# Values of an attention stage: from moving operand to stationary operand in two column halves of TensorE

## The chip, the cores and the metric

The kernel runs on one core of one Trainium2 chip. The metric is the time of one execution on the device, in microseconds (us). The kernel before takes 1840.47 us (median of 3 runs, 1840.46 to 1841.13).

## The reference, cut to what matters

One decoder block over 1024 tokens of width 1024, all in float32. Two token mixers run in parallel and are merged by gates; a feed-forward part follows.

```python
q_a, ..., q_b, k_b, v_b, iq, ik, iw, g_merge = split(rmsnorm(h) @ w_in)
# NSA: 8 heads in 2 groups of 4 that share keys and values
o_cmp = softmax(q @ kc) @ vc              # 63 compressed keys
o_slc = softmax(q @ k_selected) @ v_sel   # 8 blocks of 64 keys, chosen per query
o_win = softmax(q @ k_win) @ v_win        # the last 512 keys
y_a = g0 * o_cmp + g1 * o_slc + g2 * o_win
# DSA: 8 heads, one key and one value, 256 keys chosen per query
y_b = softmax(q_b @ k_chosen) @ v_chosen
merged = sigmoid(gA) * (y_a @ w_nsa) + sigmoid(gB) * (y_b @ w_dsa)
h = h + merged @ w_out
h = h + (silu(hn @ w_gate) * (hn @ w_up)) @ w_down
out = rmsnorm(h)
```

Selected keys are computed as dense attention with a bias of -1e30 on keys that aren't chosen.

## The kernel before, in words

The program is written by hand for each engine: every engine has its own list of instructions, and counting semaphores join them. Five stages follow one another: the input projection with the choice of DSA keys (until some 496 us), the attention (496 to 954 us), the merge, the output projection, and the feed-forward part. Only the attention and the first steps of the merge are touched.

The attention walks over 192 units. A unit is one branch (dsa, win or slc), one tile of 128 queries `i` (0 to 7), and one of 8 heads. It has n key blocks of 128 keys: n = i + 1, at most 5 for win. Summed over all units that is 816 key blocks. The loop `for u in range(STEPS6)` is written out on every engine in the same order, and each part of a unit happens a fixed number of steps later:

- step u: TensorE computes the scores of unit u into one half of `psA` (lines 1401 and 1402: the keys come as a high and a low part, each one pass). VectorE scales them, adds the bias and takes the maximum (line 1949, tile `s`).
- `E_LAG` = 1 step later: ScalarE takes the exponential and its sum (line 1188, tile `p`).
- `T_LAG` = 2: TensorE turns the n blocks of probabilities (line 1342, a transpose: the data is the stationary operand and `ident` moves) into one of two banks of `psT`, up to 4 blocks a bank. ScalarE or VectorE copies a bank to `pT` (line 602). `group` makes TensorE wait until the bank used two groups ago has been copied.
- `V_LAG` = 3: TensorE multiplies by the values (line 1517). Stationary is a block of `pT`, 128 keys by 128 queries, and the 64 columns of values move. Each such product in float32 is two instructions in the trace, each with its own weight load. All 8 heads of a query tile lie side by side in one bank of `psT`, queries on the partitions.
- `F_LAG` = 4: after the last head VectorE divides by the sums (line 1977), and GpSimd adds the branches (line 987). `Y_LAG` = 7: the sum is turned (line 1342, from `ya`) and split into a high part `yTh` by ScalarE (line 1178) and a low part `yTl` by VectorE (line 2008).

Interleaved with the units stand the compression of keys (line 1526, 64 products of 128 by 128), the scores and the output of the compressed branch for each tile (lines 1549, 1550 and 1562), and the ranking of blocks on VectorE and GpSimd. The merge has 16 steps (`m_step`), each 24 instructions with 512 moving columns; the first stands in the loop's tail, the others behind it. Step m serves output columns m // 2 and token half m % 2.

Of the kernel before, what the change touches and what calls it, by code (L numbers as in the profile page):

```python
# [28 lines left out]
F32 = mybir.dt.float32  # L29
# [7 lines left out]
P = 128  # L37
HD = 64
# [10 lines left out]
def hybrid_block(nc, A, out, scratch):  # L49
# [62 lines left out]
    v_win = sb(mix, "v_win", [P, NT, KV * HD])  # L112
    nsa_gate = sb(mix, "nsa_gate", [P, NT, 3 * H])
# [55 lines left out]
    yTh, yTl = {}, {}  # L169
    for set_ in ("nsa", "dsa"):  # L170
        yTh[set_] = sb(att, f"yTh_{set_}", [P, KT // 2, S], F32R)
        yTl[set_] = sb(att, f"yTl_{set_}", [P, KT // 2, S], F32R)
    with ExitStack() as s:
        w1c = [sb(s, f"cmp_w1_{n}", [P, JP, HH * P]) for n in "kv"]
    kT = {a: sb(att, f"kT_{a}", [P, KV, 2, S], F32R) for a in ("slc", "win")}
    work = ExitStack()
    s_sb = [sb(work, f"s{n}", [P, S]) for n in range(2)]
# [3 lines left out]
    PR = 3  # L181
    p_sb = [sb(work, f"p{n}", [P, S]) for n in range(PR)]
    pT = [sb(work, f"pT{n}", [P, NT, P]) for n in range(2)]
    ya = [sb(work, f"ya{n}", [P, H * HD]) for n in range(2)]
    yt = sb(work, "ytmp", [P, H * HD])
    c_s = sb(work, "c_s", [P, H, 64])
    c_p = sb(work, "c_p", [P, H, 64])
    c_pT = sb(work, "c_pT", [P, 4, P])
# [4 lines left out]
    cmp_a = sb(work, "cmp_above", [P, KV, NSLC, NSLC])  # L193
    cmp_b = sb(work, "cmp_equal", [P, KV, NSLC, NSLC])
# [6 lines left out]
    psum_r = sb(work, "psum_r", [P, 3, NT, H])  # L201
    work.close()
# [130 lines left out]

    Z_STEPS, G_STEPS = 8 * len(ORDER), 4 * KT
    free1 = [8 * (n // 4) + 7 if n < NCH else Z_STEPS + 2 * (n - NCH) + 1 for n in range(len(items1))]
    M_STEPS, O_STEPS, F_STEPS = 2 * KT, 2 * NT, FT
    free2 = [2 * j + 1 for j in range(KT)] + [M_STEPS + 8 * (n // 4) + 7 for n in range(8)]
# [73 lines left out]
    W2_AT = [ND + 64, ND + 72]  # L411
# [11 lines left out]
    E_LAG, T_LAG, V_LAG, F_LAG, Y_LAG = 1, 2, 3, 4, 7  # L423
    STEPS6 = len(units) + Y_LAG + 2

# [17 lines left out]


    groups6, opened = [], []
    for u in range(STEPS6):
        a, i, h = at(u - T_LAG)
        if a:
            groups6 += [("p", u - T_LAG, g) for g in range(len(seg(keys_of(a, i)[1])))]
        a, i, h = at(u - V_LAG)  # L450
        if a and h == 0:
            opened.append((a, i))
# [4 lines left out]
        for key, stage in (("cs", 0), ("cp", C_TURN), ("co", C_OUT)):  # L457
            if cmp_tile(u, stage) is not None:
                groups6.append((key, cmp_tile(u, stage), 0))
        if y_of(u):  # L460
            groups6.append(("y", *y_of(u)))
# [3 lines left out]
    def by_act(key):  # L465
        return key[0] in ("ch", "cp") or (key[0] == "p" and key[2] == 0)
# [3 lines left out]
    o_took = nth(opened)  # L470
    ysteps = nth([k for k in groups6 if k[0] == "y"])
    groups_y = list(ysteps)

# [25 lines left out]
    pv_ps, o_out, y_done, yh_done = sem("pv_ps"), sem("o_out"), sem("y_added"), sem("yh")  # L499
# [38 lines left out]
    w2.gone = [(m_ps, 2 * j + 2) for j in range(KT)]  # L538
# [38 lines left out]
    N_CONST1 = 9  # L577
    N_CONST6 = N_CONST1 + 2 + 11

    def windows(eng, n, done):  # L580

        for g in range(KV):
            src = kcvcT[HD * g:HD * (g + 1), n, :].rearrange("p (c s) -> p s c", s=CSTR)
            for u in range(2):
                for j in range(2):
                    last = eng.tensor_tensor(
                        xc[n][HD * u:HD * (u + 1), 8 * j:8 * j + 8, g, 0:NW], src[:, u::2, j:j + NW],
                        posc[n][HD * g:HD * (g + 1), CSTR * j + u:CSTR * (j + 1):2].unsqueeze(2).to_broadcast([HD, 8, NW]),
                        ALU.add)
                    last.then_inc(done, 1)  # L590

    def evac_p(eng, copy, v, act_side):

        a, i, h = at(v)
        for g, (c0, c1) in enumerate(seg(keys_of(a, i)[1])):
            key = ("p", v, g)
            if by_act(key) != act_side:
                continue
            eng.wait_ge(t_ps, g6[key] + 1)
            if v >= 2:  # L600
                eng.wait_ge(pv_ps, v - 1)
# [9 lines left out]
    def _(sp):  # L611
# [106 lines left out]
        for n in range(2 * RAW, RAW + RING):  # L718
            w2.load(sp, n)
# [1614 lines left out]
```

## Time and profile before

| | |
|---|---|
| median of 3 runs | 1840.47 us |
| the profiled execution | 1840.48 us |
| its span, first to last instruction | 1838.8 us |
| TensorE busy (matmuls) | 1707.3 us, 93% |
| VectorE, ScalarE, GpSimd busy | 66%, 38%, 31% |
| granted TensorE clock, mean | 0.97 |

A row of the profile names line, engine, operation, written tile <- read tiles, and shape. PE is TensorE's matmul side and PEld its weight loads, DVE is VectorE, ACT is ScalarE, POOL is GpSimd, SP is SyncE, which issues the DMAs. The ends of matmuls are modelled, and their intervals overlap, so what a matmul costs is read from the distance between starts. PEclk is the granted clock as a share of 2.4 GHz: 0.5 is 1.2 GHz.

### The profile page before, as it was taken

To read this page: it belongs to the slowest core of one execution; us is meant where nothing else is said; L and a number is where in the kernel's file an instruction comes from. 1 tells how busy PE (TensorE), PEld (TensorE's weight loads), DVE (VectorE), ACT (ScalarE), POOL (GpSimd) and SP (SyncE) were. 2 spreads that over 40 slices of the span, in tenths; PEclk is the share of its full clock that TensorE was granted. 3 is DMA by queue.
4 is the path that set the end of the run, shared out by engine and by line. 5 is a ranking of instruction groups with operands and counts; after the bars stand their busy time and mean duration, and the time that the engine had idled before them with its cause. 6 is when DMAs were issued, how large, how long until landed. Compare 5 with 4: busy or idle time off the path is not lost.

```text
span 1838.8 us, 25573 instructions
## 1 busy us (share of the span) xinstructions
PE 1707.3 (93%) x9248; PEld 1467.2 (80%) x9248; DVE 1208.7 (66%) x2181; ACT 701.4 (38%) x1398; POOL 567.1 (31%) x396
## 2 busy tenths in 40 slices
PE   6789989999999999999999999899999999889994
PEld 5667778888898989889988877688888888668883
DVE  6689778999243545566646516667676676458976
ACT  5543433311274457655532114422322222234443
POOL 3303232322040012322212121544454445245451
PEclk9899989999999989999999999999999999989997
DMA  5103232532242001001015523122333222853432
GB/s 178 46 12 105 71 102 73 174 92 91 50 136 115 13 24 47 12 13 35 1 44 163 169 90 120 50 94 87 123 117 104 86 87 75 297 200 98 156 102 92
DMA packets 152590, 172.21 MB, mean 94 GB/s; under 512 B 18961, under 2 KB 102929, under 8 KB 152209
## 3 DMA queue, kind: packets, MB, share of 16 engines
q1 hardware_dynamic: 152464, 170.57, 28.9%
q8 instruction: 75, 1.23, 0.3%
q14 instruction: 51, 0.41, 0.1%
HBM read 121.00 MB, written 49.55 MB: 93 GB/s over the span
## 4 chain that ended last, share of the span: by engine, by line
PE 78%; DVE 10%; ACT 3%; DMA 3%; issue 3%; POOL 1%; SPq 1%; DVEq 0%; ACTq 0%; POOLq 0%
PE psA L1335 13%; PE psA L1336 13%; PE psA L1337 13%; PE psT L1517 9%; PE psT L1342 7%; PE psT L1336 5%; PE psT L1337 5%; PE psT L1335 5%; PE psA L1402 3%; PE psA L1401 3%; DMA act_raw<-scratch_act 1%; DVE rotated L1776 1%; DVE equal L1836 1%; POOL w_lo L377 1%; DVE above L1836 1%
## 5 line engine op out<-in xcount | busy, mean ns | idle before, releaser
L377 POOL TENSOR_TENSOR w_lo<-w_raw,w_hi 128x1024 fp32r<-128x1024 f32 (+2 forms) x52 | 119.9, 2314 | 243.3 <-ACT w_hi L372 243.3
L1188 ACT ACTIVATE p<-s,nmax 128x640 f32<-128x640 f32 (+7 forms) x192 | 143.9, 750 | 121.4 <-DVE nmax L1949 120.8
L995 POOL TENSOR_TENSOR w_lo<-w_sum,w_hi 128x1024 fp32r<-128x1024 f32 x44 | 115.5, 2626 | 129.4 <-ACT w_hi L1243 129.4
L1342 PE MATMUL psT<-ident,p 128*128 128x128 f32 x816 | 131.2, 282 | 19.2 <-DVE yTl_dsa L2008 4.7
L1018 POOL TENSOR_TENSOR w_lo<-act_raw,w_hi 128x512 fp32r<-128x512 f32 x77 | 104.9, 1366 | 137.8 <-ACT w_hi L1272 137.8
L2161 DVE TENSOR_TENSOR w_lo<-wd,w_hi 128x512 fp32r<-128x512 f32 x77 | 96.5, 1257 | 66.9 <-ACT w_hi L1279 66.6
L1335 PE MATMUL psA<-w_hi,xTh 128*128 128x512 f32 (+2 forms) x320 | 124.5, 389 | 13.6 <-POOL w_lo L377 9.5
L1336 PE MATMUL psA<-w_lo,xTh 128*128 128x512 f32 (+2 forms) x320 | 120.4, 376 | 0.0
L1337 PE MATMUL psA<-w_hi,xTl 128*128 128x512 f32 (+2 forms) x320 | 120.1, 375 | 0.0
L1342 PEld LDWEIGHTS psT<-ident,p 128*128 128x128 f32 x816 | 98.8, 154 | 26.4 <-ACT p L1188 7.0
L372 ACT CAST w_hi<-w_raw 128x1024 fp32r<-128x1024 f32 (+2 forms) x52 | 52.3, 1014 | 151.0 <-PE psA L1337 108.9
L1272 ACT CAST w_hi<-act_raw 128x512 fp32r<-128x512 f32 x77 | 47.8, 621 | 151.7 <-PE psA L1337 57.2
L602 ACT COPY pT<-psT 128x512 f32<-128x512 f32 (+3 forms) x192 | 93.8, 489 | 20.7 <-PE psT L1342 20.6
L1335 PE MATMUL psA<-xTh,w_hi 128*128 128x512 f32 x256 | 100.0, 391 | 0.0
L1337 PE MATMUL psA<-xTh,w_lo 128*128 128x512 f32 x256 | 99.6, 389 | 0.0
L1336 PE MATMUL psA<-xTl,w_hi 128*128 128x512 f32 x256 | 99.6, 389 | 0.0
L602 DVE COPY pT<-psT 128x128 f32<-128x128 f32 (+3 forms) x96 | 40.8, 425 | 82.9 <-PE psT L1342 82.5
L1836 DVE TENSOR_SCALAR_CACHE_REDUCE equal<-score,bit_try 128x512 f32<-128x512 f32 (+2 forms) x93 | 93.8, 1009 | 0.0
L1243 ACT CAST w_hi<-w_sum 128x1024 fp32r<-128x1024 f32 x44 | 46.2, 1053 | 118.1 <-DVE w_sum L2103 58.1
L894 POOL TENSOR_TENSOR roped<-z,cosT 128x512 f32<-128x512 f32 (+3 forms) x48 | 40.3, 846 | 163.4 <-ACT z L1063 96.8
L2117 DVE TENSOR_TENSOR act<-gate,act 128x512 f32<-128x512 f32 x33 | 67.0, 2029 | 35.1 <-ACT gate L1283 35.1
L1335 PE MATMUL psA<-w_hi 128*128 128x512 f32 x176 | 71.5, 406 | 17.3 <-DVE w_lo L2161 11.5
(351 smaller groups left out, 4949.1 us busy)
## 6 DMA issues: line engine op xcount, KB each, us to landing
act_raw<-scratch_act SPq DMA_DIRECT2D x77, 256.0 KB, 2.6
w_raw<-in_w_in_dram SPq DMA_DIRECT2D x28, 512.0 KB, 3.8
scratch_act<-act SPq DMA_DIRECT2D x33, 256.0 KB, 2.1
scratch_act<-act_sum SPq DMA_DIRECT2D x33, 256.0 KB, 2.1
scratch_gates<-gate_out SPq DMA_DIRECT2D x32, 256.0 KB, 3.1
gates<-scratch_gates SPq DMA_DIRECT2D x32, 256.0 KB, 4.1
wd<-in_w_down_dram SPq DMA_DIRECT2D x4, 1536.0 KB, 7.7
a<-in_w_gate_dram SPq DMA_DIRECT2D x22, 256.0 KB, 3.2
```

The lines of the kernel that those rows point to most:

```text
L377: nc.gpsimd.tensor_tensor(self.lo[n % RING][:, 0:u], self.raw[n % RAW][:, 0:u], self.hi[n % RING][:, 0:u].bitcast(F32), ALU.subtract).then ...
L602: copy(pT[v % 2][:, c0 // P:c1 // P, :].rearrange("p k t -> p (k t)"), psT[:, g6[key] % 2, 0:c1 - c0])\
L995: nc.gpsimd.tensor_tensor(lo2[n % RING][:], block_of(n)[:], hi2[n % RING][:].bitcast(F32), ALU.subtract)\
L1018: nc.gpsimd.tensor_tensor(lo2[slot][:, 0:512], act_raw[n % 6][:], hi2[slot][:, 0:512].bitcast(F32), ALU.subtract)\
L1188: a_.activation(p_sb[v % PR][:, 0:n], s_sb[v % 2][:, 0:n], ACT.Exp, scale=-1.0, bias=nmax[:, BR[a], i, h:h + 1], accum_out=psum_p[:, BR[a] ...
L1335: pe.matmul(ps, ah, bh, start=first, stop=False)
L1336: pe.matmul(ps, ah, bl, start=False, stop=False)
L1337: mm = pe.matmul(ps, al, bh, start=False, stop=last)
L1342: mm = pe.transpose(bank[:, P * n:P * (n + 1)], src, ident[:])
L1517: mm = pe.matmul(bank[:, HD * h:HD * (h + 1)], pT[v % 2][:, k, :], val, start=(k == 0), stop=(k == n - 1))
L1836: done.append(signal(v_.tensor_scalar((tk_gt, tk_eq)[n % 2][:, 0:P * (i + 1)], score_of(i), threshold(n), None, ALU.is_ge, ALU.add, accum_ ...
L2161: v_.tensor_tensor(lo2[slot][:, 512:1024], wd_of(D_FROM[q])[:, k, :], hi2[slot][:, 512:1024].bitcast(F32), ALU.subtract).then_inc(dl_done, 1)
```

## The change

The order of operands in the product with the values is exchanged. The 64 columns of values are stationary, and fill one half of TensorE's columns. The turned probabilities of two neighbouring heads, 2 x 128 queries, move as 256 columns. Even key blocks use columns 0 to 63 and write partitions 0 to 63, odd ones use columns 64 to 127 and write partitions 64 to 127. The outcome is the sum over even and over odd blocks, with the head's dimension on the partitions. So it has to be turned back: ScalarE copies the bank of 4 heads to `acc`, TensorE turns 4 blocks, VectorE scales both halves into `ytmp`, and GpSimd adds the halves.

```diff
-    E_LAG, T_LAG, V_LAG, F_LAG, Y_LAG = 1, 2, 3, 4, 7
+    E_LAG, T_LAG, V_LAG = 1, 3, 1
+    O_LAG, F_LAG, Y_LAG = T_LAG + 1 + V_LAG + 1, T_LAG + 1 + V_LAG + 2, 8
+    M_AT = [len(units) + T_LAG, len(units) + O_LAG, len(units) + Y_LAG + 1]
...
+    for u in range(1, len(units), 2):
+        a, i, h = units[u]
+        n = keys_of(a, i)[1]
+        mine = [(u, k, min(2, n - k)) for k in range(0, n, 2)]
+        first = (len(mine) + 1) // 2
+        for m, job in enumerate(mine):
+            jobs_at[u + T_LAG + (m >= first)].append(len(jobs))
+            jobs.append(job)
...
         for u in range(STEPS6):
+            for j in jobs_at[u]:
+                (a, i, h), k, nk, w = of_job(j)
+                uq = jobs[j][0]
+                pe.wait_ge(p_done, uq + 1)
+                turn4(group(("p", j, 0)), [s_sb[v % SR][:, P * c:P * (c + 1)] for c in range(k, k + nk) for v in (uq - 1, uq)])\
+                    .then_inc(t_ps, 1)
...
-            v = u - V_LAG
-            a, i, h = at(v)
-            if a:
+            for j in jobs_at[u - V_LAG]:
+                (a, i, h), k, nk, w = of_job(j)
...
-                for k in range(n):
...
-                    mm = pe.matmul(bank[:, HD * h:HD * (h + 1)], pT[v % 2][:, k, :], val, start=(k == 0), stop=(k == n - 1))
-                mm.then_inc(pv_ps, 1)
+                for c in range(k, k + nk):
...
+                    rows, cols = slice(HD * (c % 2), HD * (c % 2 + 1)), slice(2 * P * (c - k), 2 * P * (c - k + 1))
+                    mm = pe.matmul(bank[rows], val, pT[j % PT][:, cols], start=(c < 2), stop=(c >= n - 2))
+                if n == 1:
+                    mm = pe.matmul(bank[HD:P], zero[:], pT[j % PT][:, 0:2 * P], start=True, stop=True)
+                mm.then_inc(pj_done, 1)
...
+            if group_of(u, O_LAG):
+                o = o6[group_of(u, O_LAG)]
+                pe.wait_ge(acc_out, o + 1)
+                turn4(group(("o", *opened[o])), [acc[o % 2][:, P * k:P * (k + 1)] for k in range(G)]).then_inc(t_ps, 1)
+            if u == M_AT[1]:
+                m_step(1)
...
-            v_.tensor_tensor(heads(target[:], H), ps, r, ALU.mult).then_inc(o_out, 1)
+            v_.tensor_tensor(yt[o % 2][:].rearrange("p h r d -> p h (r d)"),
+                             psT[:, g6[key] % 2, :].rearrange("p (h c) -> p h c", h=G), r, ALU.mult).then_inc(t_dve, 1)
```

A job is the turning and copying of up to two key blocks of two heads, at most 512 columns; ScalarE copies the even jobs and VectorE the odd ones. A pair's jobs are shared out over two steps. What else changes: the exponential writes over `s`, now 6 buffers; `pT` has 8. For the second half of the tokens ScalarE copies the turned sum raw to `y_raw`, and splits it at the end into `yTh` and `yTl` in 4 pieces for each mixer. The merge begins with three steps of the first token half (`MSEQ`). SyncE no longer waits for the last product before it loads the merge's gates, but only for the last output of the compressed branch and the last ranking. GpSimd builds the compression's inputs in four pieces inside the loop.

In TensorE's list, two steps of slc units in query tile 7 (n = 8) read as follows before. `p` are probabilities, `ident` the unit matrix, `kT_slc` keys, `pT` turned probabilities.

```order
L1342 MATMUL psT<-ident,p2 128x128 x8
L1401 MATMUL psA<-kT_slc,q1 128x512
L1402 MATMUL psA<-kT_slc,q1 128x512
L1401 MATMUL psA<-kT_slc,q1 128x512
L1402 MATMUL psA<-kT_slc,q1 128x512
L1517 MATMUL psT<-v_slc,pT0 128x64 x8
L1342 MATMUL psT<-ident,p0 128x128 x8
```

At the same place in the changed kernel the end of a step and the start of the next read as follows; `s` holds the probabilities.

```order
L1474 MATMUL psA<-kT_slc,q1 128x512
L1589 MATMUL psT<-pT0,v_slc 64x256 x2
L1589 MATMUL psT<-pT1,v_slc 64x256 x2
L1414 MATMUL psT<-ident,acc1 128x128 x4
L1414 MATMUL psT<-ident,s0 128x128
L1414 MATMUL psT<-ident,s1 128x128
L1414 MATMUL psT<-ident,s0 128x128
L1414 MATMUL psT<-ident,s1 128x128
```

Where a step had 8 products with 64 moving columns, it has 4 with 256 (two jobs of two key blocks, for two heads); behind every second pair stand 4 further transposes, of `acc`, and then the next step's begin.

The loop's tail in TensorE's list before, behind the last scores (`w2_hi0` is the first merge weight):

```order
L1342 MATMUL psT<-ident,p1 128x128 x8
L1517 MATMUL psT<-v_slc,pT1 128x64 x8
L1342 MATMUL psT<-ident,p2 128x128 x8
L1517 MATMUL psT<-v_slc,pT0 128x64 x8
L1517 MATMUL psT<-v_slc,pT1 128x64 x8
L1335 MATMUL psA<-yTh_nsa,w2_hi0 128x512
```

And in the changed kernel, from the end of the first merge step to the start of the second:

```order
L1409 MATMUL psA<-yTh0_dsa,w2_lo0 128x512
L1589 MATMUL psT<-pT4,v_slc 64x256 x2
L1589 MATMUL psT<-pT5,v_slc 64x256 x2
L1589 MATMUL psT<-pT6,v_slc 64x256 x2
L1589 MATMUL psT<-pT7,v_slc 64x256 x2
L1414 MATMUL psT<-ident,acc1 128x128 x4
L1407 MATMUL psA<-yTh0_nsa,w2_hi1 128x512
```

The first merge step moved ahead of the last values, and the second ahead of the last sum `ya`, whose four transposes stand between the second and the third.

## Rows read from the trace of the kernel before

**Rows 1.** The page: busy time, slices, and the chain by line.

```profile
PE 1707.3 (93%) x9248; PEld 1467.2 (80%) x9248; DVE 1208.7 (66%) x2181; ACT 701.4 (38%) x1398; POOL 567.1 (31%) x396
...
PE psA L1335 13%; PE psA L1336 13%; PE psA L1337 13%; PE psT L1517 9%; PE psT L1342 7%; PE psT L1336 5%; PE psT L1337 5%; PE psT L1335 5%; PE psA L1402 3%; PE psA L1401 3%; DMA act_raw<-scratch_act 1%; DVE rotated L1776 1%; DVE equal L1836 1%; POOL w_lo L377 1%; DVE above L1836 1%
```

**Rows 2.** Engines' busy time in stretches of the attention; PEclk follows the engines.

```profile
496.00:540.00 44.00, 41.22 (x311) 39.42 (x312) 20.79 (x76) 34.65 (x103) 23.59 (x29) 0.92 0.60 157
540.00:658.00 118.00, 111.59 (x907) 106.05 (x907) 56.55 (x118) 56.21 (x109) 2.09 (x2) 1.00 0.14 55
658.00:700.00 42.00, 39.63 (x295) 38.76 (x294) 21.69 (x88) 26.45 (x99) 7.96 (x7) 0.84 0.06 17
700.00:948.00 248.00, 239.53 (x1937) 228.53 (x1935) 145.84 (x360) 143.86 (x308) 52.05 (x76) 0.99 0.06 20
```

**Rows 3.** TensorE in time, units of n = 8: start, length, line, shape, count.

```profile
936.13 0.40 PE L1402 MATMUL psA<-kT_slc,q 128*128 128x512 f32 x1
936.36 1.90 PE L1517 MATMUL psT<-v_slc,pT 128*128 128x64 f32 x16
938.09 1.05 PE L1342 MATMUL psT<-ident,p 128*128 128x128 f32 x8
938.90 0.47 PE L1401 MATMUL psA<-kT_slc,q 128*128 128x512 f32 x1
939.21 0.39 PE L1402 MATMUL psA<-kT_slc,q 128*128 128x512 f32 x1
939.43 0.39 PE L1401 MATMUL psA<-kT_slc,q 128*128 128x512 f32 x1
939.67 0.40 PE L1402 MATMUL psA<-kT_slc,q 128*128 128x512 f32 x1
939.90 1.90 PE L1517 MATMUL psT<-v_slc,pT 128*128 128x64 f32 x16
941.63 1.05 PE L1342 MATMUL psT<-ident,p 128*128 128x128 f32 x8
942.52 1.90 PE L1517 MATMUL psT<-v_slc,pT 128*128 128x64 f32 x16
```

**Rows 4.** Groups of the attention by shape: busy us, mean ns, then idle before.

```profile
L1342 PE MATMUL psT<-ident,p 128*128 128x128 f32 x816 | 131.2, 282 | 19.2 <-DVE yTl_dsa L2008 4.7 <-DVE yTl_nsa L2008 4.7 <-DVE ya L1984 3.1
L1517 PE MATMUL psT<-v_slc,pT 128*128 128x64 f32 x576 | 74.1, 275 | 0.0
L1517 PE MATMUL psT<-v_b,pT 128*128 128x64 f32 x576 | 73.3, 273 | 0.0
L1517 PE MATMUL psT<-v_win,pT 128*128 128x64 f32 x480 | 63.6, 275 | 0.0
L602 DVE COPY pT<-psT 128x512 f32<-128x512 f32 x16 | 11.1, 692 | 18.3 <-PE psT L1342 18.3
L602 ACT COPY pT<-psT 128x512 f32<-128x512 f32 x120 | 68.2, 568 | 12.9 <-PE psT L1342 12.9
L1977 DVE TENSOR_TENSOR ytmp<-psT,psum_r 128x512 f32<-128x512 f32 x16 | 11.0, 686 | 2.6 <-PE psT L1517 2.6
```

**Rows 5.** The chain of waits, 544 to 563 us: a long piece of 128 instructions.

```profile
547.42 14.36 PE psT L1526 x128
```

**Rows 6.** TensorE in time: products with 64 moving columns in one pass.

```profile
625.12 0.28 PE L1550 MATMUL psT<-k_cmp,q 128*128 128x64 f32 x1
625.23 0.28 PE L1549 MATMUL psT<-k_cmp,q 128*128 128x64 f32 x1
```

**Rows 7.** All engines in time, the loop's tail: TensorE's wait behind the first merge step.

```profile
954.22 0.60 PE L1342 MATMUL psT<-ident,ya 128*128 128x128 f32 x4
954.85 0.58 ACT L1178 CAST yTh_nsa<-psT 128x512 fp32r<-128x512 f32 x1 [9.37 <-PE psT L1342]
955.47 0.69 DVE L2008 TENSOR_TENSOR yTl_nsa<-psT,yTh_nsa 128x512 fp32r<-128x512 f32 x1 [5.87 <-ACT yTh_nsa L1178]
956.22 0.50 PE L1335 MATMUL psA<-yTh_nsa,w_hi 128*128 128x512 f32 x1 [1.40 <-DVE yTl_nsa L2008]
```

More of the change, by code:

```diff
@@ L332, in hybrid_block @@
     tg = {k: n for n, k in enumerate(tgroups)}
+    MSEQ = [(j, 0) for j in range(3)] + [(j, 1) for j in range(3)]
+    MSEQ += [(j, half) for j in range(3, KT) for half in range(2)]
+    m_last = [MSEQ.index((j, 1)) for j in range(KT)]
     Z_STEPS, G_STEPS = 8 * len(ORDER), 4 * KT
@@ L442, in y_of, with group_of @@
         return (a, i) if a in ("slc", "dsa") and h == H - 1 else None
+    def group_of(u, lag):
+        a, i, h = at(u - lag)
+        return (a, i, h // G) if a and h % G == G - 1 else None
+    jobs, jobs_at = [], {u: [] for u in range(-1, STEPS6)}
+    last_job, pair_jobs = {}, {}
+    for u in range(1, len(units), 2):
[6 more added lines that the diff above has]
+            jobs.append(job)
+        last_job[a, i, h // G] = pair_jobs[u - 1] = pair_jobs[u] = len(jobs) - 1
     groups6, opened = [], []
     for u in range(STEPS6):
-        a, i, h = at(u - T_LAG)
-        if a:
[L449 to L452, printed above, removed]
+        groups6 += [("p", j, 0) for j in jobs_at[u]]
         if u == CH_AT:
@@ L537, in hybrid_block @@
             w1.gone.append((g_ps, 2 * (n - NCH) + 2))
-    w2.gone = [(m_ps, 2 * j + 2) for j in range(KT)]
+    w2.gone = [(m_ps, m + 1) for m in m_last]
     frees = 0
@@ L575, in heads, with windows, of_job @@
         return ap.rearrange("p (h d) -> p h d", h=n)
-    N_CONST1 = 9
+    N_CONST1 = 10
     N_CONST6 = N_CONST1 + 2 + 11
-    def windows(eng, n, done):
+    def windows(eng, n, u, done):
         for g in range(KV):
             src = kcvcT[HD * g:HD * (g + 1), n, :].rearrange("p (c s) -> p s c", s=CSTR)
[L584 to L592, printed above, removed]
-        a, i, h = at(v)
[L595 to L601, printed above, removed]
-            copy(pT[v % 2][:, c0 // P:c1 // P, :].rearrange("p k t -> p (k t)"), psT[:, g6[key] % 2, 0:c1 - c0])\
-                .then_inc(t_act if act_side else t_dve, 1)
+            for j in range(2):
+                eng.tensor_tensor(
+                    xc[n][HD * u:HD * (u + 1), 8 * j:8 * j + 8, g, 0:NW], src[:, u::2, j:j + NW],
+                    posc[n][HD * g:HD * (g + 1), CSTR * j + u:CSTR * (j + 1):2].unsqueeze(2).to_broadcast([HD, 8, NW]),
+                    ALU.add).then_inc(done, 1)
+    def of_job(j):
+        u, k, nk = jobs[j]
+        return units[u], k, nk, nk * 2 * P
     def roped(q, col, w):
@@ L963, in _ @@
         for u in range(STEPS6):
+            if u in X_AT:
+                n, r = X_AT.index(u) // 2, X_AT.index(u) % 2
+                if any(group_of(v, F_LAG) for v in range(u)):
+                    pool.wait_ge(y_done, sum(1 for v in range(u) if group_of(v, F_LAG)))
+                windows(nc.gpsimd, n, r, (cx_k, cx_v)[n])
+                pool.wait_ge((cx_k, cx_v)[n], 4 * (r + 1))
+            if u == MASKS_AT:
+                block_masks()
             i = cmp_tile(u, C_MAX)
@@ L1152, in _, with chunks_hi @@
             a_.activation(gst[g % 2][:], psA[:, g % 4, :], ACT.Sigmoid).then_inc(g_out, 1)
+        def chunks_hi(set_):
+            act.wait_ge(pj_done, len(jobs))
+            act.wait_ge(t_act, act_took["y", "dsa" if set_ == "dsa" else "slc", NT - 1])
+            for k in range(KT // 2):
+                a_.copy(yTh[set_, 1][:, k, :], y_raw[set_][:, k, :]).then_inc(yc_hi, 1)
         for u in range(STEPS6):
```

313 lines of the change are left out of this document (182 added, 131 removed).

## The prediction

> **What bounds the kernel now.** I read the page's busy times and chain first. TensorE is busy for 93% of the span, and the products with the values alone make 9% of the chain, the transposes 7% [rows 1]. Then the stretches: from 496 to 948 us TensorE's busy time is 432 of 452 us, while VectorE has 245, ScalarE 261 and GpSimd 86 [rows 2]. A busy PE includes some waiting, so I took the steps apart. In units of n = 8 one step, from value products to value products, takes 939.90 - 936.36 = 3.54 us: 1.73 for 16 value instructions (108 ns each), 0.81 for 8 transposes, 1.00 for four score products [rows 3]. Nothing stands between them. So TensorE's own work sets the pace there, and what the change does to its list decides. In that step ScalarE has one copy of 0.57 us of `pT`, VectorE one of 0.69 [rows 4], beside one exponential and one bias pass; both are covered.
>
> **Value products that go.** 576 + 576 + 480 = 1632 instructions [rows 4] by 108 ns (16 in 938.09 - 936.36) [rows 3]: -176.3 us. What do they wait for? One-pass products with the same 64 moving columns start every 110 ns [rows 6], so that distance is not the moving columns: it is the load of 128 stationary columns. The change halves the stationary side, which makes loads cheap, and lengthens the moving side to 256.
>
> **Value products that come.** 408 products and 12 with `zero` are 840 instructions, if each is two as before. Price of one with 256 columns: full float32 with 128 columns takes 14.36 / 128 = 112 ns [rows 5], and there weight load and moving side can't be told apart. The upper bound is proportional to the columns, 224 ns, which also stands next to the one-pass product of 512 columns, 939.67 to 939.90, 0.23 us [rows 3]. The lower bound is that 112 ns were all weight load, and 256 columns cost no more than that. I take 224, since two streams of 256 are one of 512. (The Trainium skill, FP8 and Floating Point Precision, section TensorE Precision Notes, has four passes for true FP32. With two instructions that is two passes in each, 512 columns, and the sum would be as with 224.)
>
> **How far the halves overlap.** If a product in one half runs beside one in the other, with starts in the list's order, a product waits only for the one before it in its own half. In a job of two blocks the list reads even, even, odd, odd (two instructions each): three time slots in place of four; two jobs in a step take five in place of eight. Counted through all 232 jobs in 168 steps that is 588 slots in place of 840. 588 x 0.224 = +131.7 us. No row shows two column halves at once, so both ends stay: 588, and 840, which is +188.2.
>
> **Sums turned back.** 48 groups of 4 transposes = 192, by 111 ns (8 in 942.52 - 941.63) [rows 3]: +21.3 us. The copies to `acc` (48 on ScalarE at some 0.57 us, a copy of this shape [rows 4]) and 48 scalings in place of 24 on VectorE at 0.69 [rows 4] lie beside TensorE, but the transposes' bank must be free. Where a step behind such a group has two jobs (n of 5 and more: 12 query tiles, 2 groups each, 24 times), the second job waits until VectorE has scaled: 0.69 us and some 0.1 of signals, of which the first job's transposes cover 0.44. 24 x 0.36 = +8.6 us. If VectorE is held up elsewhere it is double that; none if TensorE has slack there.
>
> **Changing the array's shape.** The value products now use half the columns, everything around them all. 168 steps have such products, so 336 changes of shape. The trace has none: all rows read 128*128. Below is nothing. Above: TensorE runs empty each time. A value instruction's row lasts 275 ns, of which the next hides all but 108, so emptying costs at most 167 ns [rows 3, 4]. The nearest rows are the change from transposes to plain products: 938.90 to 939.21, 0.31 us, where the next of the same kind needs 0.22 to 0.24; back from plain products to transposes the distance stays at the usual 108 ns [rows 3]. One direction costs about 0.07, the other nothing. I take that here: 168 x 0.07 = +11.8 us (0 to +56).
>
> **Waits that go.** TensorE waited 4.7 + 4.7 us for `yTl` [rows 4], about 0.8 a time; for the second token half only ScalarE's copy remains before the bank is free: -4.7. In the tail it stood 1.40 us for the last `yTl` [rows 7], and the start of the next merge step was stretched; three steps of the first half, 5.5 us each, now cover the last transposes, splits and the gates' loads: -2. The clock stood at 0.92 and 0.84 of full in 496 to 540 and 658 to 700 us [rows 2], so 16% of 44 us and 32% of 42 us at half of full speed, 20 us in all, of which 10 are lost. These are units of n = 1, where every engine waits for another. More steps of slack (`T_LAG` 3, six `s`) fill some of it, fewer value products empty it again: -4, anything from -10 to +8. Together about -11.
>
> **Taken as free.** ScalarE has at n = 8 for a pair two exponentials, two copies and half an `acc`, VectorE two bias passes, two copies and half a scaling; by the rows above both come to some 4.3 us of a pair's 6 us. GpSimd has 3 small additions for each of 32 groups and one for 16, in steps where it is idle. The raw copies and later splits of the second half move 16 VectorE and ScalarE operations to the tail, beside 11 us of merge steps. GpSimd's window pieces end before step 36 needs them. SyncE issues the gates' loads earlier, when the DMA queues are nearly empty (0.06 [rows 2]).
>
> **Sum.** -176.3 + 131.7 + 21.3 + 8.6 + 11.8 - 11 = -13.9 us. The profiled execution took 1840.48 us, the same as the median of the runs, so the sum gives 1826.6, and I say 1827. Its own range, with the switch from 0 to 0.07 in both directions and the clock's term at either end, is 1805 to 1845.
>
> **Rivals.**
> - *Every change of shape empties TensorE.* The place is each border between scores, value products and transposes, 336 in all, at 167 ns [rows 3, 4]: +56 in place of +11.8, so 1871, slower. It decides from about 0.08 us a change, where the sum crosses zero. For it speaks that weights of the one shape can hardly be loaded among products of the other. Against it, that a change of kind is free one way and cheap the other [rows 3]. (The Trainium skill, TensorEngine Tiling, section Tiling Modes, says that changing the tiling mode drains TensorE, and changing the tile does not. By that rule this rival is the forecast; no row of the trace can show it.) Chance 24%.
> - *The halves don't overlap*, because the products queue or because float32 doesn't allow it: 840 slots, +56.4, so 1883. The values then cost more than before, 188 against 176. (The Trainium skill, TensorE: Matmul & The Clock Gate, Part 3, measured three column tiles at 2.38 times one; it tells nothing of float32.) Chance 8%.
> - *256 columns cost what a load costs*, 112 ns: 588 x 0.112 = 65.9, so 65.8 less than taken, 1761. For it speaks only that rows 5 don't exclude it. Chance 10%.
> - *TensorE gets its time and loses it again to the two banks.* Every job, sum and `ya` goes through two banks of `psT`, and half of the jobs now depend on VectorE, which also has the ranking. At 0.08 us for each of 168 steps that is +13.4, so 1840, no change. For it speaks that VectorE already makes TensorE wait for `ya` and `yTl` [rows 4]; against it that a copy takes 0.57 to 0.69 us of a step of some 3. Chance 14%.
>
> **Numbers.** The forecast has 44%. A measurement of this kernel can't tell less than 0.2%, 3.7 us, from no change. Faster by more: 40 of the forecast's 44, all 10 of the cheap columns, 4 of the two banks, 54%. Within: 2 of the forecast, 2 of the emptying, 6 of the banks, 10%. Slower: 2, 22, 8 and 4, 36%. The range of eight in ten leaves out the cheap columns below and the case without overlap above, and runs from 1785 to 1876.
>
> **What would show it.** In the changed profile: value instructions of 256 columns whose starts in pairs (even beside odd) lie 0 to 10 ns apart, and some 224 ns in one half; five slots, 1.1 us, in a step of n = 8, which then takes 2.9 to 3.1 us against 3.54. From a score product to the first value product, and from the last one to the first transpose, no more than 0.07 us above the usual distance; 0.17 or more at each would show the first rival. Starts 224 ns apart throughout: no overlap. Behind `acc`'s transposes a wait for VectorE's scaling of about 0.4 us at n of 5 and more. Attention's end, 954 us now, at 941; the merge and all behind it shifted as a whole. What would make it wrong: a price of the shape's change above 0.08 us, or stretches at half clock that grow past 20 us because the units of n = 1 and 2 give TensorE less to do.

## The result, and the profile after

| kernel | median us | runs | ratio to before, 95% interval |
|---|---|---|---|
| before | 1840.8 | 1840.46 to 1845.89 (4) | 1 |
| changed | 1860.2 | 1859.06 to 1862.78 (4) | 1.0101 [1.0088, 1.0114] |

The change makes the kernel slower by 1.0%, some 19 us. I had forecast 1827, a gain of 14. The page of the changed kernel, first its busy times, then the chain by line:

```profile
PE 1707.2 (92%) x8648; PEld 1356.7 (73%) x8648; DVE 1257.4 (68%) x2225; ACT 700.5 (38%) x1378; POOL 604.8 (32%) x461
...
PE psA L1407 13%; PE psA L1408 13%; PE psA L1409 13%; PE psT L1414 8%; PE psT L1589 6%; PE psT L1408 5%; PE psT L1407 5%; PE psT L1409 5%; PE psA L1474 3%; PE psA L1473 3%; DMA act_raw<-scratch_act 1%; DVE rotated L1855 1%; DVE equal L1915 1%; POOL w_lo L390 1%; DVE above L1915 1%
```

The products with the values (L1589) fell from 9% of the chain to 6%, and the transposes (L1414) rose from 7% to 8% [rows 1]. VectorE has 49 us more, GpSimd 38. The same stretches as in [rows 2], with busy time and count of PE, PEld, DVE, ACT and POOL, and behind them the granted clock:

```profile
496.00:540.00 44.00, 39.96 (x234) 25.56 (x233) 24.00 (x83) 28.19 (x81) 25.12 (x24) 0.92 0.56 145
540.00:658.00 118.00, 111.25 (x780) 81.58 (x779) 64.00 (x127) 61.34 (x121) 10.94 (x22) 1.00 0.16 59
658.00:700.00 42.00, 34.59 (x258) 24.82 (x257) 22.75 (x85) 23.39 (x76) 11.48 (x15) 1.00 0.04 14
700.00:948.00 248.00, 227.76 (x1486) 157.42 (x1484) 166.59 (x372) 137.15 (x303) 74.10 (x115) 0.99 0.08 24
```

TensorE was busy for 432 us of these 452 before and is for 414 now. It waits. What for, in all of 490 to 1062 us (total, times, longest; an idle time of 150 ns or less isn't listed):

```profile
PE psT L1414 <- DVE ya L2058: 10.2, 8, 2.7
PE psT L1414 <- DVE ytmp L2050: 10.0, 20, 0.6
PE psA L1407 <- DVE merged L2085: 5.8, 2, 4.3
PE psT L1589 <- DVE pT L2120: 4.6, 9, 0.6
PE psT L1414 <- ACT acc L1237: 3.9, 8, 0.9
```

Before, the largest entries were 4.7 twice, for `yTl`, and 3.1 for `ya` [rows 4]. All of TensorE's listed waits from the first score product to the first output projection add up to 44.9 us, before to 21.8; those of the transposes alone to 31.9, before to 19.0. One step of n = 8, TensorE in time (the last two rows belong to the next one):

```profile
946.48 0.63 PE L1414 MATMUL psT<-ident,s 128*128 128x128 f32 x4 [0.50 <-DVE ytmp L2050]
...
947.64 0.40 PE L1474 MATMUL psA<-kT_slc,q 128*128 128x512 f32 x1
947.97 1.08 PE L1589 MATMUL psT<-pT,v_slc 128*64 128x256 f32 x8
948.99 1.09 PE L1414 MATMUL psT<-ident,s 128*128 128x128 f32 x8
949.84 0.48 PE L1473 MATMUL psA<-kT_slc,q 128*128 128x512 f32 x1
```

From values to values (947.97 to 950.94, where the next ones start) it takes 2.97 us, 3.54 before [rows 3]: the gain is there where n is large. Within the eight value instructions the records start at 943.879 and 943.885, 944.146 and 944.152, 944.362 and 944.368, 944.578 and 944.584 (the step before this one), and the next transpose at 944.894. So two halves run side by side, 6 to 7 ns apart. A pair follows a pair after 216 ns, the first after 267. The way in and the way out of the halves are longer than usual: score to value 327 ns where it was 232, value to transpose 310 where two pairs lie 216 apart. And the transpose behind that one is late as well: it starts at 945.060, 166 ns on, where transposes usually follow each other after 109. Leaving out waits and half clock, this second distance is 165 ns behind 145 of 146 stretches in the halves; before, it was that long behind 10 of 149.

I took the distance from each TensorE instruction to the next one, between the first score product and the first output projection, and added it up by the kind of the earlier one (sums over the trace's records, us; the differences are of unrounded sums):

| kind | before | changed | difference |
|---|---|---|---|
| value products | 186.6 | 132.8 | -53.8 |
| scores (way into the halves) | 120.9 | 141.1 | +20.2 |
| transposes | 108.8 | 150.8 | +41.9 |
| merge steps | 88.7 | 96.7 | +8.1 |
| rest | 37.8 | 39.8 | +1.9 |
| all | 542.9 | 561.1 | +18.3 |

A wait stands in this table under the kind ahead of it. The first stage, whose code is the same, took 2.6 us more in this profiled run, what lies behind the output projection's start 1.4.

The merge, too, lost its cover. TensorE in time, the fifth merge step's first product:

```profile
992.02 0.77 PE L1407 MATMUL psA<-yTh_nsa,w_hi 128*128 128x512 f32 x1 [4.30 <-DVE merged L2085]
```

VectorE there: the last four subtractions, and the first operation of the third merge result:

```profile
976.33 2.50 DVE L2065 TENSOR_TENSOR yTl_nsa<-y_raw_nsa,yTh_nsa 128x512 fp32r<-128x512 f32 x4 [3.02 <-ACT yTh_nsa L1204]
...
989.86 0.69 DVE L2080 TENSOR_TENSOR ma<-psA,gates 128x512 f32<-128x512 f32 x1 [7.44 <-DMA gates<-scratch_gates]
```

SyncE's issues:

```profile
981.30 0.37 SPq L378 DMA_DIRECT2D w_raw<-in_w_branch_nsa_dram  x1
...
982.81 1.93 SPq L739 DMA_DIRECT2D gates<-scratch_gates  x4
```

VectorE makes the second merge result only behind the eight subtractions, the gates of the third step are asked for at 982.8 behind a weight load, and the 4.30 us of waiting end in a stretch at half clock (989.8 to 996.6, 1.2 GHz in place of 2.4). Merge steps 2 to 4 take 25.0 us; before, three took 16.5, and the only wait above 0.3 us was the 1.40 [rows 7].

### The profile page after: what moved, and what is told of

Its sections match the earlier page's. It is cut to its first block, busy times and chain, and to the rows that moved or that the text cites. A ratio compares the mean times of both kernels' runs of the same rounds, so it can differ in the third digit from the quotient of the medians.

```text
span 1861.1 us, 24336 instructions
## 1 busy us (share of the span) xinstructions
PE 1707.2 (92%) x8648; PEld 1356.7 (73%) x8648; DVE 1257.4 (68%) x2225; ACT 700.5 (38%) x1378; POOL 604.8 (32%) x461
## 4 chain that ended last, share of the span: by engine, by line
PE 74%; DVE 12%; issue 4%; ACT 4%; DMA 3%; POOL 2%; SPq 1%; DVEq 0%; POOLq 0%; ACTq 0%
PE psA L1407 13%; PE psA L1408 13%; PE psA L1409 13%; PE psT L1414 8%; PE psT L1589 6%; PE psT L1408 5%; PE psT L1407 5%; PE psT L1409 5%; PE psA L1474 3%; PE psA L1473 3%; DMA act_raw<-scratch_act 1%; DVE rotated L1855 1%; DVE equal L1915 1%; POOL w_lo L390 1%; DVE above L1915 1%
## 5 line engine op out<-in xcount | busy, mean ns | idle before, releaser
L1260 ACT ACTIVATE s<-s,nmax 128x640 f32<-128x640 f32 (+7 forms) x192 | 144.3, 753 | 27.2 <-DVE nmax L2028 26.6
L1414 PE MATMUL psT<-ident,s 128*128 128x128 f32 x816 | 130.2, 283 | 25.9 <-DVE ya L2058 10.2
L1414 PEld LDWEIGHTS psT<-ident,s 128*128 128x128 f32 x816 | 89.8, 142 | 70.6 <-issue 58.1
L1254 ACT COPY pT<-psT 128x512 f32<-128x512 f32 (+1 forms) x116 | 64.4, 555 | 132.1 <-PE psT L1414 131.7
L2120 DVE COPY pT<-psT 128x512 f32<-128x512 f32 (+1 forms) x116 | 69.6, 600 | 55.0 <-PE psT L1414 54.2
L1344 ACT CAST w_hi<-act_raw 128x512 fp32r<-128x512 f32 x77 | 47.8, 621 | 152.1 <-PE psA L1409 57.7
```

The costliest lines, as they stand in the source:

```text
L1260: a_.activation(s_sb[v % SR][:, 0:n], s_sb[v % SR][:, 0:n], ACT.Exp, scale=-1.0, bias=nmax[:, BR[a], i, h:h + 1], accum_out=psum_p[:, BR[a ...
L1414: mm = pe.transpose(bank[:, P * n:P * (n + 1)], src, ident[:])
L2120: v_.tensor_copy(pT[j % PT][:, 0:w], psT[:, g6["p", j, 0] % 2, 0:w]).then_inc(t_dve, 1)
```

## The experiments

The ratio is to the kernel before, measured beside it; that kernel's median was 1840.8 us beside the changed one and 1842.1 to 1843.3 beside the experiments, so kernels are compared by their ratios. "This part" is the time from the first score product to the first output projection in the profiled run. "At full clock" is that time less half of what TensorE spent in it at half clock. This is an estimate, and the most that the clock can cost: a wait that falls into such a stretch isn't made longer by it.

| kernel | median us | ratio, 95% | this part us | at half clock | at full clock |
|---|---|---|---|---|---|
| before | 1840.8 | 1 | 542.9 | 23.9 | 530.9 |
| changed | 1860.2 | 1.0101 | 561.1 | 20.5 | 550.9 |
| e1 | 1863.4 | 1.0115 [1.0101, 1.0129] | 564.4 | 23.9 | 552.4 |
| e2 | 1884.0 | 1.0222 [1.0206, 1.0237] | 586.6 | 27.3 | 573.0 |
| e3 | 1859.0 | 1.0085 [1.0070, 1.0100] | 559.2 | 20.5 | 549.0 |
| e4 | 1879.4 | 1.0196 [1.0182, 1.0210] | 579.0 | 17.1 | 570.4 |
| e5 | 1856.6 | 1.0079 [1.0063, 1.0096] | 559.0 | 20.5 | 548.7 |
| e6 | 1854.0 | 1.0061 [1.0045, 1.0076] | 554.4 | 37.5 | 535.6 |
| e7 | 1850.6 | 1.0047 [1.0032, 1.0062] | 553.5 | 47.8 | 529.6 |
| e8 | 1854.2 | 1.0064 [1.0050, 1.0079] | 554.5 | 30.7 | 539.2 |
| e9 | 1864.5 | 1.0124 [1.0111, 1.0137] | 564.0 | 23.9 | 552.0 |
| e10 | 1853.3 | 1.0055 [1.0043, 1.0067] | 554.2 | 13.7 | 547.4 |
| e11 | 1826.7 | 0.9915 [0.9898, 0.9931] | 526.5 | 6.8 | 523.0 |
| e12 | 1823.1 | 0.9892 [0.9879, 0.9905] | 524.8 | 17.1 | 516.2 |
| e13 | 1831.8 | 0.9937 [0.9917, 0.9956] | 534.6 | 17.1 | 526.0 |
| e14 | 1836.5 | 0.9964 [0.9954, 0.9974] | 537.2 | 17.1 | 528.7 |

### e1: a pair's values in one step

```diff
+            values_at[u + T_LAG + V_LAG + (len(mine) > 1)].append(len(jobs))
...
-            for j in jobs_at[u - V_LAG]:
+            for j in values_at[u]:
```

> The changed kernel, with all the value products of a pair of heads in one step (the transposes of its probabilities stay in two), so that TensorE changes from products in the halves of the array and back 96 times rather than 168. No instruction is added or left out. Theory A (each change into and out of the halves costs about 95 ns, 190 ns for a step with values, which the trace of the changed kernel shows as score to first value 327 ns against 232 before, and last value to transpose 310 ns against 216 within a half): 72 x 0.19 = -13.7 us, 1846.5, and a wait of TensorE for VectorE or for a free bank takes at most 3 of it back. Theory B (a change costs the 70 ns of the prediction, and the loss lies in the new waits and the half clock): -5 us, 1855, with the waits as they were. Theory C (the steps are now uneven, four products of a pair and then none, and the scores, which wait for VectorE, can't fill the short steps): 1860 or more, with a new wait at the score products.

No gain; the ratio is 0.14% above the changed kernel's, and the two intervals overlap. The value products did fall by 10.8 us from start to start, and 72 stretches by 151 ns are 10.9. But the wait for the scaling doubled:

```profile
PE psT L1416 <- DVE ytmp L2052: 21.1, 19, 1.7
PE psT L1416 <- DVE ya L2060: 12.2, 8, 3.2
```

All of TensorE's listed waits rose from 44.9 to 64.1 us. A saved switch is worth its price only where TensorE isn't held elsewhere. None of the theories named this wait; C had the time, but put the wait at the score products.

### e2: more changes of shape

```diff
+        for m, j in enumerate(jobs_at[u - V_LAG]):
+            (later_at[u + 1] if m and j not in last_job.values() else values_at[u]).append(j)
...
+            sum_values(later_at[u])
```

> The changed kernel, with the second value job of a step (unless it is the last of its group of four heads) put behind the transposes of the next step: 56 more stretches in the halves, the same instructions. Theory A (190 ns for each stretch): 56 x 0.19 = +10.6 us, 1870.8. Theory B (70 ns): +3.9 us, 1864. Theory D (the first rival of the prediction, TensorE empties at each change and pays 167 ns each way): +18.7 us, 1879.

+22 us at full clock as well as in the runs (1.0222 less 1.0101 of 1841), 0.39 for each of 56 stretches, more than any theory. TensorE in time:

```profile
961.79 0.49 PE L1419 MATMUL psT<-ident,s 128*128 128x128 f32 x3
962.21 0.65 PE L1568 MATMUL psT<-pT,v_win 128*64 128x256 f32 x4
962.79 0.50 PE L1478 MATMUL psA<-kT_slc,q 128*128 128x512 f32 x1
```

From the last transpose to the first value it is 202 ns, where the score product came 28 ns after it: 174 more. The way in is dearer here than behind a score (+94). Two blocks side by side take 583 ns with the way out, four 1015: 216 for each of the two passes, and 151 for the stretch as a whole. 174 + 151 = 325 ns, by 56 is 18.2 of the 22. Behind the score product that follows, the next one comes 337 ns on, 315 where a transpose stood ahead: 1.2 us more. The wait for `ytmp` has the rest (12.6 us for 10.0). In the changed kernel, where transposes follow a stretch, the late second transpose (165 ns for 109) comes on top. So a stretch in the halves costs 94 + 151 + 56 = 301 ns between scores and transposes and 325 + 22 = 347 between transposes and scores, whatever its length. I had taken 70.

### e3 and e5: the merge's order, then the gates

```diff
+            if u == M_AT[1] + 1:
+                merged(1)
```

> The changed kernel, with VectorE's second merge step taken ahead of the subtractions on the second half of the turned outputs (its own subtraction of the low part stays behind them). In the trace of the changed kernel TensorE waits 1.49 us at 981.97 and 4.30 us at 992.02 for the merge. Theory A (VectorE's order there, and the gate loads that wait for it, make these waits): both go, -4 to -6 us, 1855. Theory B (the merge is late because the weights or the stretch at half clock are; the order doesn't matter): within 1 us of 1860.

2 to 3 us, of 5.8 waited, between the two theories; a wait of 3.19 us is left. e5 keeps this edit and moves the gates up:

```diff
-        for n in range(2 * RAW, RAW + RING):
+        w2.load(sp, 2 * RAW)
+        sp.wait_ge(m_done, 1)
+        load_gates(2)
+        for n in range(2 * RAW + 1, RAW + RING):
             w2.load(sp, n)
```

> The edit of e3_merge_early, and the two gate tables of the third merge step loaded ahead of the sixth block of branch weights and the gain row in SyncE's order. In the traces of the changed kernel and of e3 VectorE's third merge step starts only at 989.8, when these gates land, and TensorE's merge steps 2 to 4 take 25.0 us (23.2 in e3) where three steps take 16.5; a stretch of 6.8 us at half clock begins in them. Theory A (the gates queue on SyncE behind weight loads, which wait for GpSimd's split of the weights): steps 2 to 4 take 16.5 to 17.5 us, with or without the half clock behind a wait, 1851.5. Theory B (the half clock comes in the merge whatever the waits): 3.4 us of it stay, 1855.

Neither theory. The gates are in time now, but another wait stands in their place, and the half clock (981.4) again with it; against e3 little is won. TensorE in time:

```profile
982.15 0.76 PE L1410 MATMUL psA<-yTh_nsa,w_hi 128*128 128x512 f32 x1 [3.19 <-issue]
```

VectorE in time:

```profile
977.38 4.66 DVE L2068 TENSOR_TENSOR yTl_nsa<-y_raw_nsa,yTh_nsa 128x512 fp32r<-128x512 f32 x4
```

The wait's named releaser is "issue", but this merge step is the first of the second token half, it waits for all pieces of that half's `yTl`, and VectorE ends the last at 982.04.

### e10: four merge steps to cover the chain

```diff
-    MSEQ = [(j, 0) for j in range(3)] + [(j, 1) for j in range(3)]
+    MSEQ = [(j, 0) for j in range(4)] + [(j, 1) for j in range(4)]
...
-    W2_AT = [ND + 64, ND + 72, len(units) + 2]
+    W2_AT = [ND + 64, ND + 72, len(units) + 2, len(units) + 6]
```

> The edits of e5, and four merge steps on the first half of the tokens ahead of those on the second half, where the change has three (the fourth block of branch weights is split earlier for it). In e5 the gates were in time, and TensorE waited 3.2 us at 979 for the low parts of the last tile's turned outputs, which VectorE ended at 982.0, 8.5 us after that tile's transposes. Theory A (that chain of copy, split and subtraction is now longer than the steps that cover it): one step more covers it, the merge takes 5.5 us a step throughout, -8 us from the changed kernel, 1852, and -11, 1849, if the stretch at half clock there goes with the wait. Theory B (the wait goes on to the weights): 1856 as e5.

Theory A, with a little less than its 8 to 11 us. The 16 merge steps take 88.3 us from start to start (88.7 before the change), 5.5 each, and the stretch at half clock there is gone. This part of the time fell by 6.9 us, the ratio by 8 (1.0055 for 1.0101).

### e4: neighbours in the same half

```diff
-                    rows, cols = slice(HD * (c % 2), HD * (c % 2 + 1)), ...
+                    r, last = k // 2 % 2, (n - 1) // 2 * 2
+                    rows, cols = slice(HD * r, HD * (r + 1)), ...
```

> The changed kernel, with the two value products of one job (neighbours in TensorE's queue) in the same half of the array and the next job's two in the other half, where the change alternates from one product to the next; with one or two key blocks the second half gets the zero product. 12 zero products more. In the changed kernel two neighbours in different halves start 6 to 7 ns apart and the pair lasts 216 ns. Theory A (the queue is in order, and a product starts beside the one ahead of it only if that one is in the other half): of the four products of two jobs only the middle two overlap, three times 216 ns rather than two, and two products of a single job don't overlap: by count of jobs 432 with two blocks each, 312 of them come in twos (156 x 0.216) or alone (120 x 0.216), about +60 us, 1920. Theory B (the queue looks past a product that waits for its half): 1860 to 1865.

+17 us, not 60. With two jobs in a step the time is the same as in the changed kernel; with one it doubles. TensorE in time, two places:

```profile
603.48 1.08 PE L1590 MATMUL psT<-pT,v_b 128*64 128x256 f32 x4
...
955.06 1.09 PE L1590 MATMUL psT<-pT,v_win 128*64 128x256 f32 x8
```

Eight instructions take as long as four, though in the program the four of one half all stand ahead of the four of the other. The records start in pairs 13 ns apart from the first on. They don't name the half, but two products of one half in a row don't pair (the four of a single job take as long as eight). So a product for a free half starts ahead of those in the list that wait for the other half: theory B's queue, with a cost in single jobs that it hadn't counted. 56 steps have one job of two blocks: 56 x 0.432 = 24.2 us expected by this count, 21.6 more in the value products found. (The Trainium skill, TensorE: Matmul & The Clock Gate, Part 3, says of packed tiles that matmuls start and end strictly in program order. These rows differ: in order, the eight would take seven slots of 216 ns and 151, 1.66 us. The measurement decides.)

### e6: sums turned later

```diff
 # in TensorE's step, between the scores and the values
+            if group_of(u, F_LAG):
+                o = o6[group_of(u, F_LAG)]
+                pe.wait_ge(acc_out, o + 1)
+                turn4(group(("o", *opened[o])), ...)
 # in VectorE's, ahead of unit_scores(u)
+            if group_of(u, F_LAG):
+                scaled(*group_of(u, F_LAG))
```

> The changed kernel, with the four transposes that turn the sums back put between the scores and the values of the next step, and VectorE's scaling of them ahead of its score subtraction in that step. Nothing is added or left out. Today they come at the end of a step, one step earlier, directly in front of the transposes of the next probabilities, which need the bank again. Theory A (the two banks make waits of TensorE: 10.0 us for the scaling, 10.2 for the scaling of the compressed output, 3.9 for ScalarE's copy of the sums between 490 and 1062): 14 to 18 us of these 24 go, 1844. Theory B (VectorE is late itself, so the wait moves to the scores): within 3 us of 1860.

The waits went as theory A has it: 15.3 us less at full clock. But 17 us more were spent at half clock, so 8.5 came back, and the time fell by 7. The wait for `ya` stayed, though the sums no longer stand between the compressed output and the next transposes:

```profile
PE psT L1414 <- DVE ya L2058: 8.9, 5, 3.3
```

A new wait came, for GpSimd's sum, just ahead of a stretch at half clock (686.4):

```profile
684.59 0.66 PE L1414 MATMUL psT<-ident,ya 128*128 128x128 f32 x4 [1.62 <-POOL ya L1031]
```

### e7: both

> The edits of e1_one_step and e6_sums_turned_later together. In the trace of e1 the value products took 10.8 us less from start to start, and TensorE's wait for the scaling rose from 10.0 to 21.1 us, so nothing was won. Theory A (a stretch in the halves costs 94 ns on entry and 151 beyond 216 for each pair of products, 245 ns in all, whatever its length; e1's gain was eaten by the bank wait alone): 72 x 0.245 = -17.6 us from e6, 1828 if e6 is at 1845. Theory B (uneven steps cost it in any order): within 4 us of e6.

At full clock 6.0 us below e6 and already 1.3 below the kernel before. In the runs it was 3, since the half clock grew to 47.8 us: theory B's time, and at full clock a third of theory A's 17.6. From 658 to 700 it stands at 0.76 (0.84 before [rows 2], 1.00 in the changed kernel):

```profile
658.00:700.00 42.00, 36.92 (x212) 27.38 (x209) 20.76 (x76) 19.48 (x64) 11.02 (x14) 0.76 0.04 13
```

### e8: a quarter of the sums turned back

```diff
-  [acc[o % 2][:, P * k:P * (k + 1)] for k in range(G)]
+  [acc[o % 2][:, P * k:P * (k + 1)] for k in range(1)]
```

> The changed kernel, with one of the four transposes that turn the sums of four heads back; the other three are left out, so the scaling reads old numbers in three quarters of its bank. 144 of 192 transposes less. Theory A (they cost TensorE their 109 ns each and nothing hides them): -15.7 us, and 1 or 2 of the waits for the copy and the scaling change sign either way, 1844.5. Theory B (the chain copy, transpose, scaling is what TensorE waits for, so the freed time turns into a wait): -5 us or less, 1855.

The other three transposes of each group are left out. The time fell by 7 us, nearer to theory B's 5, but only a part of it by B's mechanism. Transposes from start to start fell by 10.0, of 15.7: the waits for `ya` and `ytmp` took 4.3 (12.8 and 11.7). The half clock took 5.1 more.

### e9: the compressed output first

```diff
-            if cmp_tile(u - 1, C_OUT) is not None:
-                cmp_out(cmp_tile(u - 1, C_OUT))
...
                 unit_scores(u)
+            if cmp_tile(u, C_OUT) is not None:
+                cmp_out(cmp_tile(u, C_OUT))
```

> The changed kernel, with VectorE's scaling of the compressed output (ya, from the bank that TensorE's next transposes want) taken right behind the score subtraction of its step, ahead of the block comparisons, where it stood behind them in the next step. Nothing is added or left out. In the trace of the changed kernel TensorE waits 10.2 us for it in 8 places (2.43, 2.73 and 2.36 in three of them), and two of the stretches at half clock (771.4 and 863.5, 3.4 us each) begin within 3 us of such a wait's end. Theory A (VectorE's order makes the wait, the wait brings the half clock): 3 us of the 10.2 stay, both stretches go, -10 us, 1850. Theory B (the half clock comes whatever the waits there): -7 us, 1853, the stretches stay or move. Theory C (VectorE is behind in these steps in any order): within 2 us of 1860.

Theory C as far as this kernel goes, and a little worse, +4 us, though the two intervals just touch. The wait moved:

```profile
PE psT L1414 <- DVE ytmp L2050: 16.2, 25, 1.8
...
PE psT L1414 <- DVE ya L2058: 4.6, 8, 1.0
```

VectorE has block comparisons, output and sums to do in the same two steps, and TensorE's next transposes want both banks. What the order alone decides is the wait for `ya`: from 10.2 to 4.6 us.

### e11 and e12: all of it

e11 has the edits of e6, e9, e10 (with those of e3 and e5 in it), and `Y_LAG` 9 for 8. e12 has e1's besides.

> The changed kernel with the edits of e6 (sums turned between scores and values of the next step), e9, e10, and the transposes of the outputs one step later, so that GpSimd's sums are done. Values stay in two steps a pair. Theory A (the swap itself costs, per the traces, +21 us of transposes, 41 us of stretches in the halves and saves 76 us of products, so with no new waits it gains 14 us on the kernel before; the waits bring the half clock): the waits and the half clock are as in the kernel before, about 1830. Theory B (the half clock takes back what the waits gave, as it did in e6, where it grew from 20.5 to 37.5 us in the attention): 1843 to 1848.

> The edits of e11 with the values of a pair in one step (e1). Theory A: 72 stretches of 245 ns less than e11, of which uneven steps took back 9 of 17.6 in e7 against e6 (at full clock 6.0 were won): -6 to -17 us from e11, so 1813 to 1824. Theory B (half clock): within 4 us of e11.

Both beat both kernels: 0.9915 and 0.9892. In e11 TensorE's longest waits between 490 and 1062 us are:

```profile
PE psT L1419 <- DVE pT L2121: 5.2, 4, 2.2
PE psT L1419 <- DVE ya L2063: 4.1, 5, 1.6
PE psT L1419 <- DVE c_s L1973: 2.3, 6, 0.4
```

and from 700 to 948 us the clock stands at 1.00:

```profile
700.00:948.00 248.00, 236.17 (x1561) 165.54 (x1560) 164.86 (x363) 140.07 (x295) 77.66 (x116) 1.00 0.07 22
```

Its one stretch at half clock is that at 500.6, which the kernel before has too. Its kinds from start to start, against the kernel before: values -58.9, scores +18.0, transposes +22.5. TensorE's listed waits add up to 19.3 us in e11, 21.8 in the kernel before. e12 won 6.8 more at full clock, and gave 5.1 back to the clock; its time fits both of its theories.

### e13 and e14: one edit undone

> e11 with the edit of e9 undone: VectorE scales the compressed output in the next step again, behind the block comparisons. Theory A (this wait of TensorE, 2 to 3 us in each of three or four tiles, brings stretches at half clock): about 5 us of waits and 10 to 17 us at half clock (5 to 8 us lost) come back, +10 to +13 us from e11, 1838. Theory B (alone it was worth nothing, e9, and the half clock in e11 has other causes): within 3 us of e11, 1827.

> e11 with the transposes of the outputs back one step earlier (8 steps behind the scores, not 9). Theory A (in e6 and e7 TensorE waited 4 to 5 us there for GpSimd's sums, 1.62 us of them just ahead of a stretch at half clock at 686.4): +4 us of waits and one stretch of 6.8 us (3.4 lost), +7 us from e11, 1834. Theory B (only the waits): +4, 1831.

e13 lost 4 to 5 us, between its theories: waits for `ya` rose from 4.1 to 8.9 us (those for `pT` fell from 5.2 to 2.2), half clock from 6.8 to 17.1. The same edit that cost 4 us in the changed kernel (e9) brings 4 once the sums are out of its way. e14 lost 9 to 10, theory A and more:

```profile
PE psT L1419 <- POOL ya L1034: 2.5, 3, 1.6
PE psT L1419 <- POOL ya L1029: 1.9, 3, 0.9
```

and 10 us more at half clock, from 663.4 and from 683.9, as in e6.

## Why the prediction was wrong

- **The swap itself came out about as priced, by luck: two errors nearly cancel.** The values come in 232 slots of two passes, 232 x 2 x 0.216 = 100.2 us, where I had 588 single slots, 131.7: I let the list's order (even, even, odd, odd) hold a product up, and e4 shows that it doesn't. The width's price was right, 216 ns for 224. The changes of shape cost 168 x 0.245 = 41.2 us for 94 ns on the way in and 151 in the stretch, the same at every n, and 150 x 0.056 = 8.4 us at the second transpose behind it, together 49.6, not 11.8. I had bounded a stretch by twice 167, and taken one fifth of that from a row on another kind of change. Slots and changes are 149.8 against my 143.5, so 6 of the miss are here.
- **Rival "every change empties TensorE".** Its price was nearly right: 301 of 334 ns between scores and transposes, 49.6 us for its 56. My own sign of being wrong came true, a change above 0.08 us (49.6 / 336 is 0.15). But alone it would not have made the kernel slower, since the slots gave 31.5 back. (The Trainium skill, TensorEngine Tiling, section Tiling Modes, says that a change of mode drains TensorE. The trace agrees that there is a price on both borders, 94 ns more on the way in, 310 ns for 216 on the way out; that it is a drain, no row shows.)
- **The sums turned back** cost 192 x 0.109 = 20.9 us (21.3 forecast) and the bank 10.0 (8.6). Right.
- **The step that failed is "waits that go", -11, with "taken as free".** With the bank's +8.6 and without the clock's -4, my waits came to +1.9 us; TensorE's listed waits rose by 23.1, from 21.8 to 44.9. `yTl`'s fell from 9.4 to 3.0 us (I had -4.7), of which 2.4 came back as waits for the raw copies. But `ya`'s rose by 7 to 10.2: VectorE scales it behind the block comparisons. With the sums moved away it is still 8.9 (e6), with this scaling ahead of the comparisons 4.6 (e9), and undoing that edit alone brings 4.1 back to 8.9 (e13 against e11). The copy to `acc` made 3.9 and VectorE's copies to `pT` 6.1 us of new waits, and the merge took 8 us more in place of 2 less. These 21 us, the 6 of the swap, 2 of the clock and 1 outside this part are 30 of the 33 to 34 us from 1827 to 1860; the rest is open. That the waits decided is shown from the other side: with them taken away and nothing of the swap changed, the kernel is at the forecast's 1827 (e11). 8.5 us of that are less half clock than before, where I had 4, so this meeting is luck in part; at full clock e11 is 7.9 us below the kernel before, and my terms without the clock come to 9.9.
- **The rival of the two banks** had the mechanism that decided, and nearly its size at the transposes: 13.4 us, where the listed waits ahead of transposes rose by 12.9. It left out 5.0 us of waits ahead of the values and the merge. I had VectorE at 4.3 us of a pair's 6 for the common pair, and did not look at the pairs in which comparisons, output and sums fall together.
- **The clock**: -4 forecast; half of 20.5 less half of 23.9 is -1.7 in the changed kernel by the estimate above, and its variants go from -8.5 (e11) to +12.0 (e7). It is the term that hides what an edit brings.
- **No overlap, and cheap columns**: refuted by the pairs 6 to 7 ns apart and the 216 ns.
- **The forecast's own range** is added up wrong: a change from 0 to 0.07 us in both directions and the clock from -10 to +8 give 1809 to 1850 around 1827, not 1805 to 1845. The measured 1860 lies outside both.

## What to carry to other kernels

A stretch of products in halves of TensorE costs a fixed price, here 0.3 us, so make few and long ones, and put them behind score products rather than transposes. When TensorE's work is made shorter, list for each bank of PSUM who frees it and what stands ahead of that instruction on its engine in the busiest step, not in the mean one: here the new waits, 23 us, were more than the 14 to be gained. Judge edits at full clock, and together: three that alone brought -7, +4 and -8 us brought -25 together (e14), and -34 with the outputs turned a step later (e11), all by the ratios.

## What the runs showed of the hardware

- Float32 products in two column halves overlap wholly: pairs 6 to 7 ns apart, 216 ns from pair to pair. They also do when all of one half stand ahead of all of the other in the list: eight take 1.09 us, as four of one half do (e4).
- A stretch in the halves is followed by a late second transpose, 165 ns behind the first for 109 (145 of 146 places in the changed kernel). What holds it up is open.
- Waits of TensorE come with stretches at half clock (3.4, 6.8 or 10.2 us long). From 700 us to the output projection the 16 kernels have 46 of them; 43 begin during a wait of 1.0 us or more or within 3.5 us of its end. The other three have less waiting near: 0.39 us in e13 (818.6 and 866.4), some waits of 0.3 to 0.8 us in e2 (701.4). Not every such wait brings one: at 817 in the changed kernel 2.73 us of waiting left the clock at full, while the same wait in e10, with other timing, has one. What decides between them is open.
- Four subtractions on VectorE took 4.66 us in e5 beside GpSimd's split of the weights, and 2.49 without it. That the two hold each other up was not tried by itself.
